# Attention's output gate computed by halves of the tokens and spread over 30 jobs, with PSUM banks dealt out anew

## The reference

```python
def hybrid_layer(x, w_in, w_out, g_pre, g_post, ...):
    h = rms_norm(x, g_pre)
    a_q, a_kv, a_g, b_cq, b_ckv, b_kr, c_q, c_kv, z = split_cols_2(h @ w_in)
    o_a = nsa_attention(...)              # 4 heads: compressed, selected and windowed keys
    o_b = causal_block_attention(...)     # 4 heads (mla), causal
    o_c = banded_attention(...)           # 8 heads (swa), a window of 128 keys, with sinks
    mixed = jnp.concatenate([o_a, o_b.reshape(B, T, W_B), o_c.reshape(B, T, W_C)], axis=-1) * jax.nn.silu(z)
    return x + rms_norm(mixed @ w_out, g_post)

def second_block(x, w_in, w_out, ...):
    for l in range(DEPTH_2):              # 2 layers
        x = hybrid_layer(x, w_in[l], w_out[l], ...)
    return x
```

## Time and profile before

| | |
|---|---|
| median of 3 runs | 1315.31 us (1314.8 to 1315.57) |
| span of the profiled execution, the page's | 1313.0 us |
| median less that span | 2.3 us |
| layer 0, jobs 0 to 11 / 12 to 29 / 30 to 39 | 56.1 / 43.2 / 30.1 us |
| layer 1, jobs 0 to 11 / 12 to 29 | 56.1 / 42.5 us |
| granted TensorE clock in these stretches | 1.00 |

### The profile page before, as it was taken

How to read it: one execution, slowest core, us unless ns; L and a number is a source line. 1 busy time by engine, 2 the same in 40 slices (tenths; PEclk the granted TensorE clock), 3 DMA queues, 4 the chain that set the end, 5 groups by cost and what they waited for, 6 DMA issues and landing times.

```text
span 1313.0 us, 24617 instructions
## 1 busy us (share of the span) xinstructions
PE 1266.9 (96%) x9971; PEld 772.5 (59%) x9971; DVE 698.7 (53%) x1422; ACT 417.0 (32%) x904; POOL 398.1 (30%) x470
## 2 busy tenths in 40 slices
PE   5999999999999999999999999999999999999997
PEld 3454655555656666687445885446645786455553
DVE  4356567847234444573473563247646373237745
ACT  4243213253433332101024002347613102236721
POOL 0100000202334443181432320225761250115671
PEclk9999999999999999999999999999999999999999
DMA  9710112011130100042426315110004415100001
GB/s 308 288 64 0 67 66 80 26 39 65 66 130 3 67 3 3 2 153 104 147 74 137 97 32 192 65 53 1 2 16 98 135 33 192 65 1 2 1 1 64
DMA packets 71535, 96.59 MB, mean 74 GB/s; under 512 B 27639, under 2 KB 35247, under 8 KB 71422
## 3 DMA queue, kind: packets, MB, share of 16 engines
q1 hardware_dynamic: 71050, 94.76, 21.7%
q10 hardware_dynamic: 372, 0.27, 0.1%
HBM read 92.89 MB, written 2.13 MB: 72 GB/s over the span
## 4 chain that ended last, share of the span: by engine, by line
PE 85%; DVE 6%; SPq 3%; ACT 3%; issue 1%; DMA 1%; POOL 0%; DVEq 0%; POOLq 0%; ACTq 0%
PE PS L147 81%; PE PS L2830 2%; DVE AR L2936 2%; ACT AR L3058 1%; SPq L187 1%; DMA bias_rows<-AR 1%; DVE AR L2923 1%; SPq L304 1%; SPq L308 1%; ACT AR L3068 0%; SPq L309 0%; SPq L312 0%; DVE AR L2106 0%; DVE AR L866 0%; PE PS L2164 0%
## 5 line engine op out<-in xcount | busy, mean ns | idle before, releaser
L147 PE MATMUL PS<-AR 64*64 64x64 f32 (+13 forms) x9334 | 1196.2, 326 | 21.8 <-ACT AR L3068 6.0
L147 PEld LDWEIGHTS PS<-AR 64*64 64x64 f32 (+5 forms) x9334 | 703.0, 152 | 485.1 <-issue 384.7
L3058 ACT ACTIVATE AR<-AR 128x257 f32<-128x257 f32 (+5 forms) x160 | 84.9, 531 | 96.1 <-DVE AR L2936 86.1
L2936 DVE CUSTOM_DVE_ANT_0 AR<-PS,AR 128x257 f32<-128x257 f32 (+5 forms) x160 | 72.2, 451 | 60.5 <-PE PS L147 43.0
L412 POOL TENSOR_TENSOR AR<-AR 128x1 f32<-128x1 f32 (+4 forms) x26 | 21.9, 841 | 258.6 <-DVE AR L407 211.8
L1189 DVE SCALAR_TENSOR_TENSOR AR<-AR 128x441 f32<-128x441 f32 (+2 forms) x96 | 78.6, 819 | 15.7 <-ACT AR L1146 12.0
L3119 POOL TENSOR_SCALAR AR<-AR 128x257 f32<-128x257 f32 (+5 forms) x96 | 53.4, 556 | 75.8 <-DVE AR L2942 70.3
L1612 DVE TENSOR_TENSOR AR<-PS,AR 128x256 f32<-128x256 f32 x60 | 25.5, 424 | 85.7 <-PE PS L147 82.4
L3117 POOL TENSOR_SCALAR AR<-AR 128x128 f32<-128x128 f32 (+3 forms) x64 | 39.0, 609 | 68.4 <-DVE AR L2942 64.5
L2053 POOL TENSOR_TENSOR AR<-AR 128x512 f32<-128x512 f32 x36 | 49.6, 1377 | 29.0 <-DMA AR<-in_w_o 26.0
L1738 ACT ACTIVATE AR<-PS 128x512 f32<-128x512 f32 x48 | 28.7, 597 | 82.5 <-PE PS L147 80.3
(11 more groups left out here) (264 smaller groups left out, 964.8 us busy)
## 6 DMA issues: line engine op xcount, KB each, us to landing
AR<-in_w_in SPq DMA_DIRECT2D x16, 2048.0 KB, 9.1
AR<-in_w_mod SPq DMA_DIRECT2D x6, 2048.0 KB, 13.1
AR<-in_w_out SPq DMA_DIRECT2D x4, 2048.0 KB, 13.0
AR<-in_x SPq DMA_DIRECT2D x8, 512.0 KB, 5.1
AR<-in_w_in SPq DMA_DIRECT2D x4, 1024.0 KB, 7.4
AR<-in_w_o SPq DMA_DIRECT2D x2, 2048.0 KB, 8.2
AR<-in_w_in SPq DMA_DIRECT2D x2, 1664.0 KB, 8.7
AR<-in_w_in SPq DMA_DIRECT2D x12, 256.0 KB, 4.2
```

The source lines that it names most:

```text
L147: return t.matmul(o, l, r, start=s, stop=p, skip_group_check=True)
L2936: v.do.tensor_tensor_reduce(PB[j % NJP][e][:, 0:nk], ps["s", l, j, e][:, 0:nk], bias_for(qb, kind, 2 * a + e, nk), 1.0, 3e38, ALU.add, ALU ...
L3058: a_.do.activation(P, P, ACT.Exp, bias=mn[:, j % NJS, e:e + 1], scale=-1.0, accum_out=su[:, j % NJS, e:e + 1]).then_inc(sa, na("p", l, j, e))
```

## The change

Each of the six filled tiles is computed in two halves, tokens 0 to 255 and 256 to 511, as 8 matmuls of 128x256 each, into the first 256 columns of a bank. The first halves fill jobs 0 to 11, still four matmuls in each, in banks 5 and 2 by turns. The second halves fill jobs 12 to 29: 3, 3 and 2 matmuls in three jobs, a tile every three jobs, all in bank 2. Tanh and multiply go by halves too. The banks:

| jobs | scores before | scores after | transposes before | transposes after | gate before | gate after |
|---|---|---|---|---|---|---|
| 0 to 12 | 0, 1 | 0, 1 | 3, 4 | 3, 4 | 5, 2 | 5, 2 (job 12: 2) |
| 13 to 30 | 2, 0, 1 | 5, 0, 1 | 5, 3, 4 | 3, 4 | none | 2 |
| 31 on | 2, 0, 1 | 5, 0, 1 | 5, 3, 4 | 2, 3, 4 | none | none |

The marks that free the weights' slots move to the second halves of tiles 4 and 2, POOL's wait before the sums of the output weights to the second half of tile 2.

```diff
--- before.py
+++ after.py
@@ -2564,18 +2564,33 @@
         x = mm(t.go, ps["sz", l, m][:, :], w[:, i, 128 * (m % 4):128 * (m % 4) + 128], hT2[:, i, :], i == 0, i == 7)
         if i == 7:
             x.then_inc(st, nt("sz", l, m))
-            if m in (4, 2):
+
+    def half_gate(t, l, m, half, i):
+
+        k = W2 + 10 * l + 7 - m // 4
+        w, = weights(t, k)
+        if i == 0:
+            ps.take(t, "sz", l, m, half, bank=2 if half else (2, 5)[m % 2])
+        x = mm(t.go, ps["sz", l, m, half][:, 0:256], w[:, i, 128 * (m % 4):128 * (m % 4) + 128], hT2[:, i, 256 * half:256 * half + 256], i == 0, i == 7)
+        if i == 7:
+            x.then_inc(st, nt("sz", l, m, half))
+            if (m, half) in ((4, 1), (2, 1)):
                 nt.mark("weights", k)
 
-    def out_gate_v(v, l, m):
-        z = SZ[:, m, :]
-        v.wait_ge(sa, na["sz", l, m])
-        v.do.scalar_tensor_tensor(out=z, in0=z, scalar=1.0, in1=ps["sz", l, m][:, :], op0=ALU.add, op1=ALU.mult).then_inc(sv, nv())
-        ps.empty(sv, nv, "sz", l, m)
-
-    def out_gate_a(a_, l, m):
-        a_.wait_ge(st, nt["sz", l, m])
-        a_.do.activation(SZ[:, m, :], ps["sz", l, m][:, :], ACT.Tanh, bias=0.0, scale=0.5).then_inc(sa, na("sz", l, m))
+    def gate_of(l, m, *half):
+        n = 256 if half else 512
+        return SZ[:, m, 256 * sum(half):256 * sum(half) + n], ps[("sz", l, m) + half][:, 0:n]
+
+    def out_gate_v(v, l, m, *half):
+        z, p = gate_of(l, m, *half)
+        v.wait_ge(sa, na[("sz", l, m) + half])
+        v.do.scalar_tensor_tensor(out=z, in0=z, scalar=1.0, in1=p, op0=ALU.add, op1=ALU.mult).then_inc(sv, nv())
+        ps.empty(sv, nv, "sz", l, m, *half)
+
+    def out_gate_a(a_, l, m, *half):
+        z, p = gate_of(l, m, *half)
+        a_.wait_ge(st, nt[("sz", l, m) + half])
+        a_.do.activation(z, p, ACT.Tanh, bias=0.0, scale=0.5).then_inc(sa, na("sz", l, m, *half))
 
     def two_v(v, l):
         nv.mark("at", f"layer{l}")
@@ -2743,14 +2758,15 @@
     NJ, PER = len(JOBS), 10
     TURN, PV = 4, 6
     CMP_EXP, CMP_SUM, CMP_TURN, CMP_PV = 1, 2, 5, {1: 0, 4: 1}
-    GATES = [(m, i) for m in (5, 4, 1, 0, 3, 2) for i in range(8)]
-    PER_JOB = 4
-    FILLED = len(GATES) // PER_JOB
+    GATE_TILES = (5, 4, 1, 0, 3, 2)
+    GATES = [(m, half, i) for half in range(2) for m in GATE_TILES for i in range(8)]
+    FIRST_JOBS, FILLED = 12, 30
 
     def gates_in(i):
 
-        x = GATES[PER_JOB * i:PER_JOB * i + PER_JOB]
-        return x, [m for m, k in x if k == 7]
+        j, k = divmod(max(0, i - FIRST_JOBS), 3)
+        x = GATES[4 * i:4 * i + 4] if i < FIRST_JOBS else GATES[48 + 8 * j + 3 * k:48 + 8 * j + min(8, 3 * k + 3)]
+        return x, [(m, half) for m, half, k in x if k == 7]
 
     GROUP = ({"slc": 0, "win": 0, "mla": 2}, {"swa": 0})
 
@@ -2792,8 +2808,8 @@
 
     def attn_t(t, l):
         meet(t, f"qkv{l}")
-        few = itertools.cycle((0, 1)), itertools.cycle((3, 4))
-        all_ = itertools.cycle((2, 0, 1)), itertools.cycle((5, 3, 4))
+        rings_of = ((itertools.cycle((0, 1)), itertools.cycle((3, 4))), (itertools.cycle((5, 0, 1)), itertools.cycle((3, 4))),
+                    (itertools.cycle((5, 0, 1)), itertools.cycle((2, 3, 4))))
 
         def score(j):
             qb, kind, a = JOBS[j]
@@ -2885,11 +2901,11 @@
                     product_cmp(qb, CMP_PV[at])
 
         def filled(i):
-            for m, k in gates_in(i)[0]:
-                out_gate(t, l, m, k, bank=(2, 5)[m % 2])
+            for m, half, k in gates_in(i)[0]:
+                half_gate(t, l, m, half, k)
 
         for i in range(NJ + PV):
-            rings = few if i <= FILLED else all_
+            rings = rings_of[(i > FIRST_JOBS) + (i > FILLED)]
             if i % 2 == 0:
                 turned(i), filled(i), scored(i), summed(i)
             else:
@@ -2980,8 +2996,8 @@
 
         out_gate_v(v, l, 6)
         for i in range(NJ + PV):
-            for m in gates_in(i - 1)[1] if i else ():
-                out_gate_v(v, l, m)
+            for x in gates_in(i - 1)[1] if i else ():
+                out_gate_v(v, l, *x)
             if i % 2 == 0:
                 turned(i)
             qb, at = divmod(i, PER)
@@ -3075,8 +3091,8 @@
                 expo(i)
             if i % 2:
                 turned(i)
-            for m in gates_in(i)[1]:
-                out_gate_a(a_, l, m)
+            for x in gates_in(i)[1]:
+                out_gate_a(a_, l, *x)
             qb, at = divmod(i, PER)
             if qb < 4 and at == CMP_EXP:
                 expo_cmp(qb)
@@ -3123,7 +3139,7 @@
             qb, at = divmod(i, PER)
             nc = 8 * qb + 7
             if i == SUMS[0]:
-                g.wait_ge(st, nt["sz", l, 3])
+                g.wait_ge(st, nt["sz", l, 2, 1])
             if at == 0:
                 g.wait_ge(sv, nv["minc", l, qb])
                 g.do.tensor_tensor(Pc[:, :, 0:nc], Pc[:, :, 0:nc], mnc.unsqueeze(2).to_broadcast([128, 4, nc]), ALU.subtract).then_inc(sg, ng("subc", l, qb))
```

## The result

The change makes the kernel slower by 0.3%: a median of 1318.95 us (1317.54 to 1321.13) beside 1315.2 us, ratio 1.0032, 95% interval 1.0021 to 1.0044. The profiled execution took 1317.54 us with a span of 1315.7 us, 2.7 us over the span before.

The account below looks back on a forecast made before the run. PE was taken as the bound, busy 96% of the span. New waits 18.0, old ones -11.9 and width +0.7 gave +6.8 us: span 1313.0 to 1319.8, plus 2.3 for the median, 1322.1 us; range 1313 to 1328, the forecast's own 1317 to 1328.

Parts of the forecast that it names:

- hand-overs of one bank: Six a layer, jobs 11 to 26: PE waits for tanh and multiply to free the gate's bank; 7.15 us a layer.
- transposes on two: Jobs 25 to 30: with two banks the third transposed tile waits for the first one's copy; 1.85 us a layer.
- The new waits: Hand-overs and transposes' waits in attention of both layers together: 2 x (7.15 + 1.85) = 18.0 us added.
- The old waits: PE's eighteen waits in jobs 12 to 29 of both layers, 11.9 us, all taken as gone; floor half.
- the term of what goes: Moved gate work in jobs 12 to 29 covers PE's old waits, -11.9 us over both layers.
- The width: Gate matmuls at 128x256 instead of 128x512, 48 a layer in two layers: +0.7 us.
- From span to median: Median of the runs taken as 2.3 us above the profiled span, turning 1319.8 into 1322.1 us.
- The stages: Layer 0: jobs 0 to 11 near 35.5 us, jobs 12 to 29 near 67; under 64 would show the forecast wrong.
- One for one: Rival, chance 0.18: hand-overs of about 0.6 us, new waits equal old ones, no change, 1315.1 us.
- Faster: Rival, chance 0.12: hand-overs hide behind products and transposes, new waits under 5.6 us a layer; -7.5 us, 1307.8.
- Slower still: Rival, chance 0.10: in jobs 0 to 11 every pair of jobs waits for DVE's minimum; 4.5 us more, 1326.6.
- the sum was 1319.2: Skill's bank rule read plainly: each hand-over costs the evacuation alone, 0.95 us, 5.7 us for six; total 1319.2.

Follow-up runs that it names:

- e_width: Against the kernel before: gate tiles by halves, all in jobs 0 to 11, eight 128x256 matmuls a job, banks of before from job 13; 1314.03 us.
- e_044: The change with second-half matmuls spread 0, 4, 4 over each three jobs instead of 3, 3, 2; 1310.32 us, ratio 0.9966 to the kernel before.
- e_odd: The change with second halves filling odd jobs only, from job 13, 8, 4 and 4 matmuls in turn; 1310.90 us, ratio 0.997 to the kernel before.
- e_turn3: The change with the third bank moved from scores to transposes in jobs 13 to 30, second halves still in bank 2; 1322.0 us.
- e_late: The change with DVE's multiply of second halves ending in even jobs moved behind the next job's two minimums; 1329.56 us.
- e_two_banks: The change with second halves in banks 5 and 2 by turns, scores on 0 and 1 alone; 1313.75 us.

## Why the prediction was right, and where it was off

The side and the cause were right: slower, by hand-overs of one bank and by transposes on two. The time came out 3.2 us below the 1322.1 forecast.

**The new waits** hold one by one (us in the issue):

| place | forecast | layer 0 | layer 1 |
|---|---|---|---|
| after job 11 | 1.3 | 1.29 | 1.29 |
| after job 14 | 1.5 | 1.72 | 1.72 |
| after job 17 | 1.7 | 1.64 | 1.64 |
| after job 20 | 0.6 | 0.25 | 0.25 |
| after job 23, transposes and gate | 1.35 + 0.5 | 1.55 + 0.42 | 1.56 + 0.42 |
| after job 26 | 0.2 | 0.13 | 0.18 |
| transposes at 25-26, 27-28, 29-30 | 0.45, 0.5, 0.9 | 0.80, 0.65, 0.97 | 0.45, 0.65, 0.97 |
| sum | 9.0 | 9.42 | 9.13 |

**The old waits** went, 6.33 and 5.70 us, as taken (11.9); the transposes' 1.15 us at jobs 27 and 28 is in there, and the 0.65 that is left of it stands in the table.

**The step that failed is the term of what goes.** It counted only PE's waits, 11.9 us; what went was 12.03 + 4.0 = 16.0. A pair of scores whose second bank comes late loses the wait and, beside it, the array's other half, and the 4.0 us of eight such pairs are in no view of waits, since PE is busy meanwhile. With them 18.55 - 12.03 - 4.0 is +2.5, where the span grew by 2.7. The trace of the kernel before had it: job 13's scores in two pieces 1.03 us apart. The Trainium skill, TensorEngine Tiling (Array Packing), section Gotcha 1: PSUM Pressure, says that different row tiles write to different banks and can't share one at a time. No run here puts both scores of a pair into one bank; what the trace shows is the price of a second bank that comes late, 1.66 against 0.63 us.

**The width**, +0.7 forecast, was not there: e_width stands at -0.85 us, not told apart from zero.

**From span to median** I added 2.3 us, which was the median's place before. For the change the median lies 3.2 us above the profiled span: the profile has no fall of the clock, the median about one. So of the 3.7 us that the change loses at the median, 2.3 lie between its undisturbed executions (1317.5) and the kernel before, and some 1.4 are the clock's. I had not foreseen the second. The 2.3 alone is under the 2.6 us that the prediction set as the mark of what can be told from no change; that the median passed it is in part the clock's doing, and luck.

**The stages.** I said I would be wrong if jobs 12 to 29 came under 64 us in layer 0, and they came at 63.91, with jobs 0 to 11 at 38.5 instead of 35.5. That mark was badly set: my sum left out that the first hand-over and the fills cross the cuts. Taken together, less job 0's fill, the stages are 100.7 against 35.5 + 67 = 102.5, and the 1.8 us between are about what that layer's score pairs gave back, 2.0.

**The rivals.** One for one needed hand-overs of 0.6 us and had 0.13 to 1.72. Faster needed new waits under 5.6 us a layer; they are over 9. But its point of decision was wrong in the same term: with the pairs in it the change breaks even near (11.9 + 4.0) / 2 = 8 us, and e_044 (4.73) and e_odd (4.03) lie under either. Slower still did not come: in jobs 0 to 11 still only two pairs of scores wait for the minimum, 0.56 each, at 823.18 and 828.79.

By the Trainium skill's rule on banks (Perfetto Trace Analysis, section Optimizing Tensor Performance) the sum was 1319.2, nearest to what came. Its reading, 0.95 us for every hand-over, is not what the trace shows: the six are 0.13 to 1.72 us, and their sum of 5.45 only happens to be near 5.7. Besides, that sum lacks the transposes' wait at job 24 (1.55 us a layer) as well as the score pairs' gain (2.0 us a layer), and the two nearly cancel: the nearness is luck. As advice it holds: with two banks rotating, the gate's waits fell from 5.45 us to none.

## What to carry over

Work that fills gaps needs a bank that is free when the fill begins: put a whole job between two tiles in the same bank, and the same halves in the same banks turn from 0.3% slower to 0.34% faster. When a wait is to be filled or removed, look also for what runs beside what because of it: a pair on two halves of the array that slips apart costs time while PE counts as busy. And follow what stands behind a wait before paying for its removal; in e_turn3 the next wait took nearly its whole place, 1.88 us for 1.55 + 0.42.

## What the runs showed of the hardware

TensorE's granted clock can fall to 1.2 GHz for a little over 3 us in the middle of a busy stage, in some executions of a program and not in others. In the changed kernel a fall costs 1.7 us; PE is busy throughout it (2.90 of 2.90 us from 1203.20). Falls also lie in the profiles of e_late (from 864.1 us, behind a wait of 2.79 us), e_two_banks (from 917.9, behind 0.97 and 0.95) and e_width (1183.6 to 1187.0, behind waits like those of the kernel before). Behind the 2.78 us of e_late's layer 1 there is none. The kernel before seems to have them too, at a smaller price, though its profile shows none: four of its executions with a mean granted clock of 0.994 took 1315.1 to 1315.8 us, beside a median of 1314.88. The eleven executions of e_044 and e_odd stand at 0.997 or 0.998 throughout. So long waits of PE are not all that it takes, and what brings a fall about stays open. The Trainium skill, TensorE: Matmul & The Clock Gate, section "A second HAM failure mode: psum-queue depth-cycling", tells of a kernel whose cycling through PSUM banks idled PE often enough for the clock to swing between its levels. No run here shows whether the falls above are of that kind.
